# Token rows that reach the experts and come back through a scratch in memory

## The reference, cut to what matters

```python
def moe_ffn(x, w_router, b_router, w_gate, w_up, w_down):
    logits = (x @ w_router) + b_router
    top_vals, top_idx = lax.top_k(logits, TOP_K)          # TOP_K = 2 of 8
    weights = jax.nn.softmax(top_vals, axis=-1)
    gates = jnp.sum(jax.nn.one_hot(top_idx, 8) * weights[..., None], axis=-2)
    out = jnp.zeros_like(x)
    for e in range(8):
        out = out + gates[..., e:e + 1] * swiglu(x, w_gate[e], w_up[e], w_down[e])   # 1024 -> 1792 -> 1024
    return out
```

## Time and profile before

| what | value |
|---|---|
| median of 3 runs | 1063.82 us (1062.89 to 1063.83) |
| the profiled execution | 1064.27 us, its span 1062.2 us |
| PE busy | 1035.2 us, 97% |
| DVE, ACT busy | 774.8 us (73%), 636.1 us (60%) |
| bytes by DMA | 265.13 MB, mean 250 GB/s |
| a round of experts | gathers start at 588.78, 654.05, ... 980.38 us |

### The profile page before, as it was taken

The page is one execution under the profiler, slowest core; times in us unless marked ns, Lnnn a source line. Parts: engine busy times, 40 slices in busy tenths (PEclk is TensorE's granted clock), DMA queues, the critical chain, the costliest instruction groups (busy, mean ns, idle before and its releaser), DMA issues.

```text
span 1062.2 us, 15010 instructions
## 1 busy us (share of the span) xinstructions
PE 1035.2 (97%) x5836; PEld 942.4 (89%) x5836; DVE 774.8 (73%) x778; ACT 636.1 (60%) x680; POOL 28.4 (3%) x55
## 2 busy tenths in 40 slices
PE   8999999999999999999899999999999999999996
PEld 6987889999999998888798898989989899898995
DVE  4557565465456648666588898988889888898886
ACT  4655454433444545455467776877767777676864
POOL 1201000000000000000100000000000000000000
PEclk9999999999999999999599999999999999999998
DMA  9744666565563674335269899999999989899892
GB/s 317 215 145 145 206 194 207 168 208 170 176 231 120 228 179 131 128 119 204 94 238 340 320 343 349 325 345 329 346 321 341 352 326 344 328 351 346 314 349 93
DMA packets 131994, 265.13 MB, mean 250 GB/s; under 512 B 9330, under 2 KB 55426, under 8 KB 131955
## 3 DMA queue, kind: packets, MB, share of 16 engines
q1 hardware_dynamic: 130530, 259.80, 70.6%
q0 software_dynamic: 1424, 4.78, 1.4%
HBM read 263.52 MB, written 1.05 MB: 249 GB/s over the span
## 4 chain that ended last, share of the span: by engine, by line
PE 88%; DVE 6%; ACT 3%; issue 1%; DMA 1%; POOL 1%; SPq 0%; POOLq 0%; ACTq 0%; DVEq 0%
PE A L442 21%; PE A L443 21%; PE A L444 21%; PE S L442 5%; PE S L444 5%; PE S L443 5%; PE T L796 3%; DVE lo L1271 2%; PE T L487 2%; PE S L818 2%; PE T L847 1%; ACT hi L907 1%; DMA raw<-in_gm_w_in 1%; PE T L522 1%; ACT R L953 1%
## 5 line engine op out<-in xcount | busy, mean ns | idle before, releaser
L1271 DVE TENSOR_TENSOR lo<-raw,hi 128x1792 fp32r<-128x1792 f32 (+3 forms) x320 | 556.0, 1779 | 122.9 <-ACT hi L907 122.8
L907 ACT ACTIVATE hi<-raw 128x1792 fp32r<-128x1792 f32 (+3 forms) x320 | 464.8, 1503 | 189.7 <-PE A L444 153.1
L442 PE MATMUL A<-lo,xT_hi 128*128 128x448 f32 (+2 forms) x964 | 350.7, 364 | 2.4 <-DVE xT_lo L1302 2.4
L443 PE MATMUL A<-hi,xT_lo 128*128 128x448 f32 (+2 forms) x964 | 346.6, 359 | 0.0
L444 PE MATMUL A<-hi,xT_hi 128*128 128x448 f32 (+2 forms) x964 | 346.5, 359 | 0.0
L442 PEld LDWEIGHTS A<-lo,xT_hi 128*128 128x128 f32 x964 | 181.7, 188 | 17.7 <-DVE xT_lo L1302 3.0
L444 PEld LDWEIGHTS A<-hi,xT_hi 128*128 128x128 f32 x964 | 181.5, 188 | 15.7
L443 PEld LDWEIGHTS A<-hi,xT_lo 128*128 128x128 f32 x964 | 181.7, 188 | 14.7
L442 PE MATMUL S<-lo,xT_hi 128*128 128x512 f32 x224 | 88.7, 396 | 0.0
L444 PE MATMUL S<-hi,xT_hi 128*128 128x512 f32 x224 | 87.5, 391 | 0.0
L443 PE MATMUL S<-hi,xT_lo 128*128 128x512 f32 x224 | 87.2, 389 | 0.0
(11 more groups left out here) (197 smaller groups left out, 991.0 us busy)
## 6 DMA issues: line engine op xcount, KB each, us to landing
raw<-in_moe_w_gate SPq DMA_DIRECT2D x32, 1792.0 KB, 9.0
raw<-in_moe_w_up SPq DMA_DIRECT2D x32, 1792.0 KB, 9.3
raw<-in_moe_w_down SPq DMA_DIRECT2D x32, 1792.0 KB, 9.4
raw<-in_ff_w_gate SPq DMA_DIRECT2D x8, 1408.0 KB, 6.2
raw<-in_ff_w_up SPq DMA_DIRECT2D x8, 1408.0 KB, 6.0
raw<-in_ff_w_down SPq DMA_DIRECT2D x8, 1408.0 KB, 6.2
raw<-in_gm_w_in SPq DMA_DIRECT2D x10, 1024.0 KB, 5.2
raw<-in_w_mem_kv SPq DMA_DIRECT2D x8, 1024.0 KB, 5.9
```

The source lines that it names most:

```text
L442: nc.tensor.matmul(out, stat[0], mov[1], start=start, stop=False)
L443: nc.tensor.matmul(out, stat[1], mov[0], start=False, stop=False)
L907: return nc.scalar.activation(out, in_, ACT.Copy)
L1271: nc.vector.tensor_tensor(piece(lo, SPLIT, u, i), piece(raw, RAW, u, i), piece(hi, SPLIT, u, i).bitcast(F32), ALU.subtract).then_inc(lo_do ...
```

## The change

The gather and the scatter by one-hot matmul go. Instead there is a scratch `slots` in device memory of 18 blocks of 128 rows by 1024 numbers (512 KB each). One GpSimd indirect DMA per token tile and choice (four in all) writes each token's row to the place of its expert and slot. In each round ACT loads one such block with an ordinary DMA into `xrow`, and PE turns it with 8 transposes (`turn_rows`); at the head of the round ACT copies the round before's output to `yrow` and stores it with a DMA to `slots`, one block behind the inputs. In the last round GpSimd gathers each token's two result rows with four indirect DMAs, and DVE adds them with their gates after the loop (`add_rows`). The last expert's output still goes through `selT` and `scatter`, made before the loop from `sel_end`. During the dense layer SP stores zeros to the 18 blocks, one after each of 18 weight loads.

```diff
+BLOCKS = 2 * E + 2
+PER_T, PER_S = 6, 2
...
+    slots = nc.dram_tensor("slots", (BLOCKS, P, D), F32, kind="Internal").ap()
+    slot_rows = slots.rearrange("b p d -> (b p) d")
...
+        xrow, yrow = R1[:, 0:D], R1[:, D:2 * D]
...
+        rows_n = R2[:, :].rearrange("p (t d) -> p t d", t=NT)
+        y_from = [[R2[:, 0:D], R2[:, D:2 * D]], [R3[:, 2 * ECH:2 * ECH + D], GB1[:, :]]]
...
+            clear_after = [u for gu, dn in U_FF for u in (*[v for pair in gu for v in pair], *dn)][:BLOCKS]
             for u in range(3, U_MOE):
                 load(u, units[u][0])
+                if u in clear_after:
+                    b = clear_after.index(u)
+                    sp.wait_ge(zero_set, 1)
+                    sp.dma_start(slots[b].rearrange("p (a c) -> p a c", c=NT * P),
+                                 sel[:, :].bitcast(F32).unsqueeze(1).to_broadcast([P, D // (NT * P), NT * P])
+                                 ).then_inc(zero_in if b else y_stored, 16)
...
-            pe.wait_ge(moe_const, 1)
-            for c in range(2):
-                pe.wait_ge(s_free[(S_MOE + c) % 2], (S_MOE + c) // 2)
-                last = nc.tensor.matmul(S[(S_MOE + c) % 2][:, :], selT[:, 0:P], ys[0][:, c * 512:(c + 1) * 512],
-                                        start=True, stop=True)
-            last.then_inc(scat_done, 1)
...
+            def turn_rows(tj, ve):
+
+                pe.wait_ge(xrow_in, ve * 16 + 16)
+                for b in range(2):
+                    j = tj + b
+                    pe.wait_ge(t_free[j % 2], ve * PER_T + 2 * (j // 2))
+                    for i in range(4):
+                        last = nc.tensor.transpose(T[j % 2][:, i * P:(i + 1) * P],
+                                                   xrow[:, (4 * b + i) * P:(4 * b + i + 1) * P], ident[:, :])
+                    last.then_inc(t_done, 1)
...
-                scatter(0, ve)
-
-                def second_scatter():
-                    scatter(1, ve)
-                    for t in range(NT):
-                        j = t1 + t
-                        pe.wait_ge(t_free[j % 2], ve * 8 + 2 * (j // 2))
-                        nc.tensor.transpose(T[j % 2][:, 0:P], sel[:, t * P:(t + 1) * P].bitcast(F32),
-                                            ident[:, :]).then_inc(t_done, 1)
-
-                hidden_expert(ve, (U + 2, U + 3), A_MOE + 1, second_scatter)
+                hidden_expert(ve, (U + 2, U + 3), A_MOE + 1, nothing)
...
-                pe.wait_ge(sel_done, ve + 2)
                 with pe.If(ve < rounds - 1):
-                    gather(t1 + 6, ve)
+                    turn_rows(t1 + 4, ve)
...
+            act.wait_ge(route_mm, 1)
+            for t in range(NT):
+                nc.scalar.activation(rows_n[:, t, :], xn[:, t, :], ACT.Copy, scale=scaled(N_FN[1], t)
+                                     ).then_inc(rows_ready, 1)
...
+            def output_rows(c, ve):
+
+                act.wait_ge(used, ve * MU + U_MOE - 1 + c)
+                if c == 0:
+                    act.wait_ge(y_stored, ve * 16 + 16)
+                act_copy(yrow[:, c * 512:(c + 1) * 512], S[(S_MOE + c) % 2][:, :]
+                         ).then_inc(s_free[(S_MOE + c) % 2], 1)
...
-                output_hi(0, ve)
-                output_hi(1, ve)
+                output_rows(0, ve)
+                output_rows(1, ve)
+                for b in range(2):
+                    act.wait_ge(s_free[b], ve + S_MOE // 2 + 1)
+                act.dma_start(slots[bass.ds(ve, 1)].rearrange("b p d -> p (b d)"), yrow).then_inc(y_stored, 16)
...
-                for t in range(NT):
-                    j = t1 + t
-                    act.wait_ge(t_done, ve * 8 + j + 1)
-                    act_copy(selT[:, t * P:(t + 1) * P], T[j % 2][:, 0:P]).then_inc(t_free[j % 2], 2)
...
+                act.wait_ge(xg_in, 16 * 2 * NT)
+                act.wait_ge(t_done, ve * PER_T + T_MOE + 2)
+                act.dma_start(xrow, slots[bass.ds(ve + 2, 1)].rearrange("b p d -> p (b d)")).then_inc(xrow_in, 16)
...
+            def add_rows(k, t):
+
+                step(nc.vector.scalar_tensor_tensor(h[:, t, :], y_from[k][t], gate_row[:, k, t:t + 1],
+                                                    h[:, t, :], ALU.mult, ALU.add))
...
+            rowv, rowk = rt[:, 6], rt[:, 7:9]
+            step(nc.vector.tensor_scalar(rowv, slot_of[:, :, :], P - 0.5, float(P * (E - 1)), ALU.is_gt, ALU.mult))
+            step(nc.vector.tensor_tensor(rowv, rowv, slot_of[:, :, :], ALU.add))
+            step(nc.vector.scalar_tensor_tensor(rowv, pr, -float(P), rowv, ALU.mult, ALU.add))
+            for k, oh in enumerate((oh1, oh2)):
+                step(nc.vector.tensor_tensor(rowk[:, k], oh, rowv, ALU.mult))
+                step(nc.vector.tensor_reduce(rowf[:, 0, k], rowk[:, k], AX.X, ALU.add))
+            nc.vector.tensor_scalar(row_to[:, :, :], rowf[:, 0], float(P * (E + 1)), None, ALU.add
+                                    ).then_inc(row_to_set, 1)
+            step(nc.vector.tensor_scalar(r1[:, 8, 1:2], r1[:, 7, 1:2], float(P), -float(P), ALU.mult, ALU.add))
+            step(nc.vector.tensor_scalar(rowf[:, 1], rowf[:, 0], r1[:, 8, 1:2], None, ALU.is_lt))
+            nc.vector.tensor_copy(row_kept[:, :, :], rowf[:, 1]).then_inc(row_from_set, 1)
+            step(nc.vector.tensor_tensor(gate_row[:, :, :], rowf[:, 1], r1[:, 5:7, :], ALU.mult))
+            step(nc.vector.tensor_tensor(r1[:, 0, :], oh1[:, :, E - 1], r1[:, 5, :], ALU.mult))
+            step(nc.vector.tensor_tensor(r1[:, 1, :], oh2[:, :, E - 1], r1[:, 6, :], ALU.mult))
+            step(nc.vector.tensor_tensor(gate_last[:, :], r1[:, 0, :], r1[:, 1, :], ALU.add))
...
-                output_lo(0, ve)
-                output_lo(1, ve)
                 split(U + 2, ve)
-                add_outputs(0, ve)
                 split(U + 3, ve)
-                add_outputs(1, ve)
                 split(U + 4, ve)
                 multiply(0, ve, t1)
                 split(U + 5, ve)
-                dve.wait_ge(t_done, ve * 8 + t1 + 2)
-                one_hot(ve + 1)
...
+            dve.wait_ge(y_back, 16 * 2 * NT)
+            for k in range(2):
+                for t in range(NT):
+                    add_rows(k, t)
+            output_lo(0)
+            output_lo(1)
+            add_outputs(0)
+            add_outputs(1)
...
-            for a in (selT[:, :], ys[0], ys[1]):
-                last = nc.gpsimd.memset(a.bitcast(F32), 0.0)
-            last.then_inc(moe_const, 1)
+            pool.wait_ge(zero_in, 16 * (BLOCKS - 1))
+            pool.wait_ge(y_stored, 16)
+            pool.wait_ge(rows_ready, NT)
+            pool.wait_ge(row_to_set, 1)
+            for k in range(2):
+                for t in range(NT):
+                    pool.indirect_dma_start(slot_rows, bass.IndirectOffsetOnAxis(row_to[:, k, t:t + 1], 0),
+                                            rows_n[:, t, :], None).then_inc(xg_in, 16)
+            pool.wait_ge(row_from_set, 1)
+            pool.wait_ge(route_done, 1)
+            rounds = pool.value_load(nround[0:1, 0:1], min_val=E, max_val=2 * E)
+            pool.wait_ge(xg_in, 16 * 2 * NT)
+            pool.wait_ge(y_stored, rounds * 16 + 16)
+            step(nc.gpsimd.tensor_tensor(row_from[:, :, :], row_to[:, :, :], row_kept[:, :, :], ALU.mult))
+            for k in range(2):
+                for t in range(NT):
+                    pool.indirect_dma_start(y_from[k][t], None, slot_rows,
+                                            bass.IndirectOffsetOnAxis(row_from[:, k, t:t + 1], 0)
+                                            ).then_inc(y_back, 16)
```

More of the change, by code:

```diff
@@ L1215, in _ @@
             gathered_hi(T_MOE, 0)
+            act.wait_ge(rows_ready, NT)
+            act.wait_ge(sel_turned, 1)
+            act_copy(selT[:, :], S[S_MOE % 2][:, 0:NT * P]).then_inc(selT_set, 1)
             act.wait_ge(route_done, 1)
@@ L1240, in _ @@
                 with act.If(ve < rounds - 1):
-                    gathered_hi(t1 + 6, ve)
+                    gathered_hi(t1 + 4, ve)
                     split(U, ve + 1)
                     split(U + 1, ve + 1)
-            output_hi(0, rounds)
-            output_hi(1, rounds)
+            output_hi(0)
+            output_hi(1)
             for t in range(NT):
@@ L1249, in _ @@
                     s = S_MOE + 2 + 2 * t + c
-                    act.wait_ge(s_free[s % 2], rounds * 3 + s // 2 + 1)
+                    act.wait_ge(s_free[s % 2], rounds * (PER_S // 2) + s // 2 + 1)
                 if t:
@@ L1642, in _ @@
             times_gain(1, GB1)
-            step(nc.vector.memset(gate_of[:, :, :], 0.0))
-            step(nc.vector.memset(slot_of[:, :, :], -1.0))
             def bc(a):
@@ L1684, in _, with one_hot @@
             dve.wait_ge(a_free[j % 2], 2 * (j // 2 + 1))
-            step(nc.vector.tensor_scalar(slot_of[:, :, E:2 * E], slot_of[:, :, 0:E], -1e4 - P, None, ALU.add))
```

(20 more changed lines are left out.)

111 lines of the change are left out of this document (62 added, 49 removed).

## The result

The changed kernel takes 1057.73 us (median of 6 runs, 1053.83 to 1060.53), the kernel before, run beside it, 1063.33 us (6 runs, 1062.89 to 1063.83). The ratio is 0.995, 95% interval [0.993, 0.9969]: about 0.5% faster. The forecast was 1050 us. The direction is right; of the 13.8 us foretold, 5.6 came.

The account below looks back on a forecast made before the run. PE bounds the kernel before; after the change DMA and the ring of three set the rounds. 1064.3 - 22.2 (rounds) + 5.8 (GpSimd's rows) + 2.0 (tail) = 1049.9, less 0.45 for the median: 1050 us with rounding, range 1033 to 1070.

Parts of the forecast that it names:

- PE's work of a round: In the experts' rounds, PE's work falls from 65.27 to 60.55 us without gather and scatter matmuls.
- The mechanism: In the experts' rounds, DMA and the ring, not PE, set the end; 61.5 to 63.5 us a round.
- The ring's term: Three raw slots for expert loads: 14.9 us for three units, 59.6 a round, 62.5 with ACT's DMAs; 22.2 us gained.
- 2.9 for ScalarE's bytes: ACT's store and load in each round delay landings by 1.44 us each, 2 x 1.44 added to 59.6.
- the ends: GpSimd's eight indirect DMAs beside the first and last rounds: 0 to 11.9 us lost, 5.8 taken.
- the tail: VectorE's four additions after the loop, between the last lo and `output_lo`: 0 to 5.1 us lost, 2.0 taken.
- inside the 62.5: ACT's way from the hi of U through the two copies: some 0.7 us late, counted within the 62.5 us round.
- The zeros: 18 stores in the dense layer: DMA share from 0.57 to 0.78, no time lost; 29 us if every store showed.
- DMA full, and slower: Rival for the rounds: engines carry 352 to 358 GB/s at most, rounds 65.5 us, 1081 us in all; chance 0.26.
- PE stays the bound: Rival for the rounds: engines give 383 GB/s whenever asked, rounds 60.6 us, 1031 to 1036 in all; chance 0.20.
- ScalarE holds up: Rival: a DMA issue keeps ACT a microsecond or more; 62.8 us a round, 1046 in all; chance 0.12.

Follow-up runs that it names:

- half_best: Changed kernel with expert units loaded in two halves, GpSimd's gathers held until unit U+6, ScalarE's output copies and store behind U+2's split: 1033.18 us, ratio 0.9715.
- small_both: Changed kernel with ScalarE's store and load of a round carrying 128 of the 1024 columns: 1051.27 us, ratio 0.987.
- half_before: Kernel before the change, with each expert unit loaded by two DMAs of half of it: 1063.92 us, ratio 1.0002.
- two_loads: Changed kernel with ScalarE's load of a round issued twice, once into a spare tile: 1065.2 us, ratio 1.0018.
- half_loads: Changed kernel, expert units loaded in two halves, the first issued early in five of twelve units, ScalarE starting when the first lands: 1036.35 us, ratio 0.9746.
- half_start: Changed kernel, expert units loaded in two halves, both issued after the whole old lo, ScalarE starting when the first lands: 1041.98 us, ratio 0.9792.
- half_issue: Changed kernel, expert units loaded in two halves, the first issued early in five of twelve units, ScalarE waiting for both: 1041.41 us, ratio 0.9796.
- late: Changed kernel with GpSimd's four gathers held until unit U+8 of the last round, additions between the two output steps: 1056.93 us, ratio 0.9926.

## Why the prediction was right in kind and wrong in size

**PE's work of a round: right.** 60.55 us counted, 60.60 measured where nothing else holds PE (`half_best`).

**The mechanism: right.** "DMA and the ring, not PE, set the end of a round": more waits for landings, PE idle behind lo, a share of 0.97 or more, as announced; the distances were not, 63.42 to 64.87 us where 61.5 to 63.5 was named. PE was idle 1.7 to 3.3 us a round in the windows (63.42 - 61.69 the least, 64.86 - 61.60 the most), where 1 to 3 was named.

**The ring's term: the step that failed.** The ring was the right bound with the wrong length. It was 14.9 us for three units, 59.6 a round, plus 2.9 for ScalarE's bytes: 62.5. Measured was 64.34. The six middle rounds therefore gave 5.5 us of span, not 6 x 2.77 = 16.6. These 11.1 us are the whole miss of the profiled execution (10.6 in its time, 1060.53 to 1049.9; the ends and the tail come to -0.2 together, the time outside the span to -0.3). That execution is the longest of the six; the median is 2.8 us shorter, some 0.35 a round if it all lies in the rounds. The way around the ring, averaged over the 72 loads of the six middle rounds (each load's issue, its landing, ScalarE's start, VectorE's start and end, and the issue of the load three units later):

| us | prediction | changed kernel |
|---|---|---|
| issue to landing | 9.3 | 9.72 |
| landed, until ScalarE starts | 0 | 0.52 |
| first hi half | 1.65 | 1.70 |
| until VectorE starts | 0 | 0.11 |
| two lo halves | 3.96 | 3.96 |
| until SP issues again | 0 | 0.10 |
| sum | 14.9 | 16.1 |
| a round, sum x 12 / 3 | 59.6 | 64.4 |

Read this table with care. In steady rounds the sum is the distance between the issues of two loads three apart, so it gives the round in any kernel: the kernel before has 16.3 and 65.3 by the same count. What tells one bound from another is how much of it is waiting. There ScalarE starts 1.31 us after the landing on average, 0.62 of them idle until PE is done; here it is 0.52 and 0.14, and issue to landing is 9.72 instead of 9.09 (means; the prediction took a median, 9.3). That this way sets the pace is shown by the experiments and not by the sum.

One unit in which nothing is in the way shows the floor of the handing over, ScalarE and VectorE in order of time, and then SP in a view of its own:

```profile
605.75 3.29 ACT L935 ACTIVATE hi<-raw 128x1792 fp32r<-128x1792 f32 x2 [2.60 <-DMA raw<-in_moe_w_up]
...
607.48 3.96 DVE L1315 TENSOR_TENSOR lo<-raw,hi 128x1792 fp32r<-128x1792 f32 x2 [1.92 <-ACT hi L935]
```

```profile
611.47 5.84 SPq L421 DMA_DIRECT2D raw<-in_moe_w_up  x2
```

From ScalarE's start to the re-issue 5.72 us, with 0.1 from the landing to that start 5.8, not 5.6. Of the 4.8 us a round between 59.6 and 64.4, the landing makes 4 x 0.42 = 1.7, these small gaps and the 0.05 on the hi half about 1.1, and the rest, 4 x 0.50 = 2.0, is ScalarE and VectorE not free when a unit lands. Some 1.5 of it is other work; some 0.5 is ScalarE waiting for PE (1.6 us in the twelve units, of which a third counts; most at U, 0.6 for the turned rows). Most of that last part sits at three places: 1.94 us at U+2, 1.54 at U, 1.06 at U+10, against 0.1 to 0.4 at the other nine. At U+2 it is this, in the changed kernel's ScalarE:

```profile
596.70 1.28 ACT L935 ACT_TABLE_LOAD   x1
598.00 1.09 ACT L935 ACTIVATE R<-S 128x512 f32<-128x512 f32 x2
599.30 0.38 ACTq L1266 DMA_DIRECT2D slots<-R  x1
599.86 3.29 ACT L935 ACTIVATE hi<-raw 128x1792 fp32r<-128x1792 f32 x2 [0.78 <-ACT R L935]
```

The prediction had seen this row of work and put it "inside the 62.5". That was wrong: in a ring, a detour of the engine that splits adds to the way like a transfer does. The 2.9 us for bytes were too much by themselves, if one goes by `small_both`: seven eighths gone gave 1.6, so all of them are some 1.9 (0.9 by the medians). The prediction laid each of ScalarE's two DMAs whole on the round, though in its own ring a delay of one landing counts a third, and only the loads under way are delayed, 9.72 / 5.36 = 1.8 of them: 2 x 1.44 x 1.8 / 3 = 1.7 as an estimate. So it had too much for bytes and nothing for handing over and other work; the two errors partly cancel and leave 1.8 a round.

**The ends: near in the sum, by luck. The tail: right.** The sum held, for first and last round together, 5.5 gained and 5.8 lost, so 0.3 lost; measured 1.2 gained up to the first `turn_rows` and 1.8 lost in the last round, 0.5. But 1.1 of the 1.2 is there before the experts begin (the first gather starts at 522.39 instead of 523.48 us; in `half_before`, with the old code up to there, at 522.54), so it differs from one execution to the next and is not the change's. The first round itself gained 0.1. Against the middle rounds, with the kernel before as measure, the first is 0.8 us longer and the last 2.7; some 3 was foretold for each. The tail was 2.0, measured 1.6; its own working gave 5.1 - 2.8 = 2.3 and was rounded down. VectorE after the last lo in the changed kernel:

```profile
1041.89 3.92 DVE L1750 SCALAR_TENSOR_TENSOR h<-R,gate_row,h 128x1024 f32<-128x1024 f32 x3
1045.85 1.28 DVE L1750 SCALAR_TENSOR_TENSOR h<-GB,gate_row,h 128x1024 f32<-128x1024 f32 x1
1047.17 1.29 DVE L1745 TENSOR_TENSOR wk_lo<-S,wk_hi 128x512 fp32r<-128x512 f32 x2
```

Four additions at 1.28 to 1.31 us, as priced, and `output_lo` starts 1.8 us after the end of PE's last down unit (1045.39).

**The zeros: right.** The window of the earlier trace rows now:

```profile
180.00:220.00 40.00, 40.00 (x275) 39.95 (x274) 22.02 (x22) 17.38 (x20) 0.00 (x0) 1.00 0.80 251
```

PE is still busy 40.00 of 40, at a share of 0.80 (0.78 was foretold). From 130 to 310 us, the stretch that the prediction named, PE is busy 177.62 of 180 us in both kernels.

**The rivals.** "DMA full, and slower" (0.26) is refuted as a mechanism: 377 and 383 GB/s were carried with the same bytes in halved loads, 369 with whole ones (`two_loads`). The prediction weighed a statement of the Trainium skill, "DMA: Bandwidth & Descriptors", Specifications, of about 358 GB/s as a core's limit. The changed kernel's rounds of 355 to 363 GB/s look like a proof of it, and are not one; 383 over a round measures otherwise. The other statement, in "Perfetto Trace Analysis", Roofline, that a core alone may go higher, agrees with the runs. "PE stays the bound" (0.20) had the right rate of transfer and lost to the ring; with the ring shortened, its 1031 to 1036 is about what `half_loads` and `half_best` measured, 1036.35 and 1033.18. "ScalarE holds up" (0.12): an issue holds ScalarE's queue 0.38 us (0.4 taken), and the wait for its own copy ahead of it 0.78. PE sees 0.6 to 0.7 us of it a round, and that only once the ring is out of the way.

## What to carry to other kernels

With a ring of n slots write down the whole way of a slot, with each hand-over and all other work of the engines on it, and divide by n. Leave the waits for the present bound out of it: what is left is the pace that the ring could keep. A bound that lies just under the present one comes into force as soon as work is taken off. A high share of DMA with waits for landings does not tell a full engine from a ring too short: take bytes away and shorten the way, one at a time, and see which moves the round. Before a change that frees the bounding engine, halve the loads, so that a slot is refilled and used in pieces: worth nothing before it (`half_before`), 21 us after it (halving together with the earlier issue and start).

## What the hardware showed that was not expected

- A share of DMA time of 0.98 was carried with 359 GB/s, one of 1.00 to 1.01 with 377 to 383. The share is not a measure of what is left to carry.
- Smaller loads, 1792 KB split into pieces of 768 to 1024 KB, didn't lower the rate: 377 GB/s against 359.
- The spread of runs follows the bound. The kernels that PE sets keep within 0.8 us (`half_loads`, `half_best`) to 2.2 (`half_before`); the changed kernel and those in which the whole load is still on the ring spread by 4 to 10 (1053.83 to 1060.53 for the changed kernel, 1058.96 to 1069.18 for `two_loads`); `half_start` and `half_issue`, almost down to PE, by 2.1 and 3.3. Why an execution falls at one end of it is open.
- An indirect DMA of 128 rows of 4 KB holds GpSimd for 0.95 to 2.46 us, and the loads issued beside four of them land some 3 to 4 us later (13.4 to 13.6 us in the changed kernel, 12.5 in `late`, against 9.2).
